# A chain of ten layers on one core: bias rows copied 64 times instead of 128, one more piece of a down projection kept back, and weight remainders moved behind a norm's rows

## The reference, cut to what matters

```python
def mixer_layer(x, ...):                       # twice
    h = rmsnorm(x, g_norm); z = h @ w_in
    o_a = diff_attention(dq, dk, dv, lam, rel_bias[:, :8])     # score + bias[bucket(k - q)]
    o_b = dilated groups, each with its own 4 bias heads       # 12 more bias heads
    o_m = memory_attention(mq, *(rmsnorm(mem, g_mem) @ w_mem_kv))
    return x + merged(o_a, o_b, o_m) @ w_out
def second_block(x, c, ...):
    for i in range(4):                          # mixers: swa, gla, fox, swa
        sh1, sc1, g1, sh2, sc2, g2 = split(silu(c) @ ada_w[i] + ada_b[i])
        x = x + g1 * mixer(modulate(rmsnorm_2(x, gain), sh1, sc1))
        h = modulate(rmsnorm_2(x, gain), sh2, sc2)
        x = x + g2 * ((silu(h @ w_g) * (h @ w_u)) @ w_down)    # 2816 inner columns
    return rmsnorm_2(x, final_norm)
```

## Time and profile before

| | |
|---|---|
| median of 3 runs | 2226.8 us (2224.5 to 2227.19) |
| the profiled execution | 2226.34 us; its span 2224.5 us |
| PE busy | 2135.0 us (96%) |
| DVE, ACT, POOL busy | 70%, 48%, 8% |
| granted TensorE clock, mean | 0.992 of full |
| DMA | 475.61 MB, mean 214 GB/s |

### The profile page before, as it was taken

How to read it: one execution, slowest core, us unless ns; L and a number is a source line. 1 busy time by engine, 2 the same in 40 slices (tenths; PEclk the granted TensorE clock), 3 DMA queues, 4 the chain that set the end, 5 groups by cost and what they waited for, 6 DMA issues and landing times. The chain is left out here.

```text
span 2224.5 us, 34008 instructions
## 1 busy us (share of the span) xinstructions
PE 2135.0 (96%) x13635; PEld 1901.5 (85%) x13635; DVE 1566.2 (70%) x2153; ACT 1078.5 (48%) x2082; POOL 184.7 (8%) x204
## 2 busy tenths in 40 slices
PE   7899999999999999999999998999999999999997
PEld 6799888878988888777999787899798899788996
DVE  6477657776776677666899677899645895667444
ACT  5354546544445555455445543454555454464342
POOL 1000000201000011011001001001000001111000
PEclk9999999999999999999999999999999999999999
DMA  9987744566876455634899434799644797425651
GB/s 303 286 260 249 242 144 147 174 229 232 258 252 225 138 164 179 217 106 130 292 348 356 162 129 142 235 363 364 208 133 143 255 355 259 150 94 177 201 182 67
DMA packets 297171, 475.61 MB, mean 214 GB/s; under 512 B 20001, under 2 KB 151531, under 8 KB 297013
## 3 DMA queue, kind: packets, MB, share of 16 engines
q1 hardware_dynamic: 286708, 441.20, 58.8%
q0 software_dynamic: 10304, 32.23, 5.0%
HBM read 465.88 MB, written 7.47 MB: 213 GB/s over the span
## 5 line engine op out<-in xcount | busy, mean ns | idle before, releaser
L150 DVE TENSOR_TENSOR wlo<-raw,whi 128x1024 fp32r<-128x1024 f32 x640 | 771.3, 1232 | 217.5 <-ACT whi L144 215.5
L144 ACT ACTIVATE whi<-raw 128x1024 fp32r<-128x1024 f32 x640 | 649.1, 1056 | 198.6 <-DMA raw<-in_ffn_w_gu 64.9
L138 PE MATMUL G<-HTh,whi 128*128 128x256 f32 x2336 | 671.7, 288 | 11.2 <-ACT pool L144 7.0
L138 PE MATMUL G<-HTh,wlo 128*128 128x256 f32 x2336 | 661.9, 283 | 0.0
L138 PE MATMUL G<-HTl,whi 128*128 128x256 f32 x2336 | 661.8, 283 | 0.0
L138 PEld LDWEIGHTS G<-HTh,whi 128*128 128x128 f32 x2336 | 448.7, 192 | 20.0 <-issue 9.7
L138 PEld LDWEIGHTS G<-HTl,whi 128*128 128x128 f32 x2336 | 448.9, 192 | 2.1
L138 PEld LDWEIGHTS G<-HTh,wlo 128*128 128x128 f32 x2336 | 448.7, 192 | 0.0
L144 ACT ACTIVATE pool<-G 128x128 f32<-128x128 f32 (+2 forms) x400 | 165.3, 434 | 507.2 <-PE G L138 449.8
L138 PE MATMUL G<-whi,HTh 128*128 128x512 f32 (+1 forms) x784 | 314.2, 401 | 24.8 <-DVE wlo L150 14.0
L138 PE MATMUL G<-whi,HTl 128*128 128x512 f32 (+1 forms) x784 | 304.3, 388 | 5.1 <-DVE HTl L158 4.8
(11 more groups left out here) (193 smaller groups left out, 2233.7 us busy)
## 6 DMA issues: line engine op xcount, KB each, us to landing
raw<-in_ada_w SPq DMA_DIRECT2D x192, 512.0 KB, 6.2
raw<-in_ffn_w_gu SPq DMA_DIRECT2D x352, 256.0 KB, 5.1
raw<-in_w_in SPq DMA_DIRECT2D x128, 512.0 KB, 4.6
raw<-in_ffn_w_down SPq DMA_DIRECT2D x88, 512.0 KB, 6.8
raw<-in_w_in SPq DMA_DIRECT2D x160, 256.0 KB, 4.6
raw<-in_swa_w_in SPq DMA_DIRECT2D x24, 512.0 KB, 5.2
pool<-mod_rows POOLq DMA_DIRECT2D x24, 512.0 KB, 6.2
raw<-in_gla_w_in SPq DMA_DIRECT2D x24, 512.0 KB, 5.0
```

The lines of the kernel that those rows point to most:

```text
L138: return self.e.matmul(out, a, b, start=start, stop=stop, skip_group_check=True) if self.e else self
L144: return self.e.activation(out, a, func, bias=bias, scale=scale, accum_out=accum) if self.e else self
L150: return self.e.tensor_tensor(out, a, b, op) if self.e else self
```

## The change: what it does

Four edits. (1) The bias table is written 64 times, and each bias tile is read by two transfers of 64 rows. (2) In a feed-forward the second down piece of unit 8 is kept back as well: `down(8)` does one piece, and `part` does the other, and no part of t = 1 stands any longer between those of t = 0; 30 matmuls of t = 1 are left behind the last one of t = 0. The stream brings the four pieces in the order that this needs, and `turning` counts from unit 8, which moves some `ada_w` pieces forward. (3) In `normed`, `rest()` and `refill` stand behind the new rows. (4) `mod_rows` is put off when all four PSUM banks of its kind are held.

```diff
-        self.scratch = nc.dram_tensor("bias_scratch", (20, P, 512), F32, kind="Internal").ap()
+        self.scratch = nc.dram_tensor("bias_scratch", (20, 64, 512), F32, kind="Internal").ap()
...
-            for kc in range(2):
-                res.append(("w", ("dn", l, v), [("dn", 0, I["ffn_w_down_2"][l][v * 256 + kc * P:v * 256 + kc * P + P, :])]))
+            for w, kc in {8: [(8, 0)], 9: [(8, 1), (9, 0), (9, 1)]}.get(v, [(v, 0), (v, 1)]):
+                res.append(("w", ("dn", l, w), [("dn", 0, I["ffn_w_down_2"][l][w * 256 + kc * P:w * 256 + kc * P + P, :])]))
...
-    return (name in ("ya", "wo", "wo2") and last == 1 or name == "dn" and last > 8 or name == "gu" and last == 0
+    return (name in ("ya", "wo", "wo2") and last == 1 or name == "dn" and last > 7 or name == "gu" and last == 0
...
-            if kk == 4 and self.modq:
+            if kk == 4 and self.modq and not all(self.gheld):
...
             self.xtok[t] = N.nx[t] + N.sq[t]
-            q, have = self.mean(t, N)
-            self.rest()
-            self.refill(4 + t)
-            r, tr = self.rstd(q, have)
+            r, tr = self.rstd(*self.mean(t, N))
...
+            self.rest()
+            self.refill(4 + t)
             if t:
...
-        self.scr.append(self.load("POOL", f"scr{k}", self.M.scratch[:, 32 * k:32 * k + 32, :],
-                                  self.btb.a[0:20, :].unsqueeze(1).to_broadcast([20, 32, 512]), [self.tbt, self.step]))
+        self.scr.append(self.load("POOL", f"scr{k}", self.M.scratch[:, 16 * k:16 * k + 16, :],
+                                  self.btb.a[0:20, :].unsqueeze(1).to_broadcast([20, 16, 512]), [self.tbt, self.step]))
...
+            evs = [(f"bias{r}", (u.name, i, k)) for k in range(2)]
+            for k in range(2):
+                src = bass.AP(self.M.scratch.tensor, h * 64 * 512 + 127 - 64 * k, [[511, 64], [1, 384]])
+                self.h_bias(r, 64 * k, src, self.scr, self.bias_free[r], evs[k])
...
-            for kc in range(2):
+            for kc in range(1 if v == 8 else 2):
                 n, lo = self.take(("dn", l, v))
...
-                for kc in range(2):
+                for kc in range(v == 8, 2):
...
-        last = ([part(0, 9, (0, 1)), part(1, 9, (0,)), part(0, 10, (0,)), part(0, 10, (1,))], [part(1, 9, (1,))],
-                [part(1, 10, (0,)), part(1, 10, (1,), l < 3)])
+        last = ([part(0, 8, (0, 1)), part(0, 9, (0, 1)), part(0, 10, (0,)), part(0, 10, (1,))], [part(1, 8, (0, 1))],
+                [part(1, 9, (0, 1)), part(1, 10, (0,)), part(1, 10, (1,), l < 3)])
```

More of the change, by code:

```diff
@@ L1112, in get_bias @@
             r = self.bias_at.pop(0)
[L1113 to L1116, removed]
+            evs = [(f"bias{r}", (u.name, i, k)) for k in range(2)]
+            for k in range(2):
+                src = bass.AP(self.M.scratch.tensor, h * 64 * 512 + 127 - 64 * k, [[511, 64], [1, 384]])
+                self.h_bias(r, 64 * k, src, self.scr, self.bias_free[r], evs[k])
+            u["bias"].append((r, evs[1]))
     def biased(self, u):
@@ L3245, in h_gate, with h_bias @@
         e.tensor_tensor(m, m, gq, ALU.add).then_inc(*self.up(added))
-    def h_bias(self, r, src, scr, free, ev):
+    def h_bias(self, r, p, src, scr, free, ev):
         e = self.e
@@ L3250, in h_bias @@
             e.wait_ge(*self.at(t))
-        e.dma_start(self.M.bias_t[:, r, :], src).then_inc(*self.up(ev, 16))
+        e.dma_start(self.M.bias_t[p:p + 64, r, :], src).then_inc(*self.up(ev, 16))
     def h_rope(self, ps, t, dst, nh, tmp, cb, full, trp, free, read, done):
```

## The result

The changed kernel takes 2235.8 us (median of 4 runs, 2234.9 to 2237.6), the kernel before in the same rounds 2225.8 us (4 runs, 2224.5 to 2227.2). The ratio is 1.0038, with a 95% interval of 1.0025 to 1.0050: slower by 10.0 us. The forecast was 2228.4 us, a gain and a loss that cancel to +2.1 us. The time lies within its range (2215 to 2237), but on the side that had a chance of 0.27, and outside the range that the prediction gave for its likeliest case alone (2222 to 2234).

A forecast was written before the change was run, and what follows sets the result against it. TensorE is busy 96%, so only its waits and lower clock count. Terms -9.3 + 6.0 + 1.2 + 2.4 + 4.0 - 2.2 = +2.1 us on 2226.3 give 2228.4 us; 8-in-10 range 2215 to 2237.

The forecast's parts named there:

- likeliest case: The forecast itself: start gain and turn losses nearly cancel, 2228.4 us, own range 2222 to 2234; chance 0.38.
- The start: Weight waits at 77.36 and 85.71 us and the slow stretch vanish with half the bias writes: -9.3 us net.
- The wait at 61.61: At the start, TensorE's 0.90 us wait for late VectorE stays and grows by about 0.7 us.
- The start wins nothing: Rival at the start: DMA engines stay full as weights take the free time; 2237.7 us, chance 0.12.
- half of the start: Rival at the start: only 6 to 7 us of the saving reaches the late pieces; 2231.4 us, chance 0.12.
- The remainder behind the rows: Turns into a feed-forward: TensorE's awaited remainder starts 2.3 us later, 0.8 comes back; +1.5 each, +6.0 over four.
- no slow clock: Rival in turns out of a feed-forward: waits of 4.4 us pass at full clock; 2222.7 us, chance 0.18.
- The kept piece: Three turns out of a feed-forward: 2.25 us wait goes, 4.4 us comes at head's third piece; +2.4, clock +4.0.
- The turns are free: Rival: postponed remainders aren't what TensorE meets last, so turns lose nothing; 2209 us, or 2214.8 breaking even; chance 0.20.
- The end: Final norm: t = 0's chain starts 2.7 us earlier relative to TensorE's end, less 0.4 for the late remainder; -2.2 us.
- I take nothing: Doubled bias reads on GpSimd stand in gaps between roots and cost nothing; bounds 0 to +2 us.

The follow-up runs named there:

- The experiment on the two halves: Changed kernel, but remainders behind the norm's rows only for the first 128 tokens, ahead of the root for the second 128: 2218.8 us, ratio 0.9964.
- the one with 58: Kernel with copies at steps 8, 18, 24, 30 and last-layer kept piece, its 40 bias reads moved from GpSimd to SyncE: 2227.2 us, ratio 0.9994.
- the changed kernel without part three: Changed kernel with `normed` as before, remainders ahead of the rows again: 2219.0 us, ratio 0.9948; run again 2217.4 us, ratio 0.9957.

## Why the prediction was right, and where it wasn't

**The start** was right: both waits and the slow stretch are gone, 10.0 us against 9.3. GpSimd's queue gave back 52.7 - 29.7 = 23.0% of 55 us of the engines, 12.7 us; half of the bias was put at 13. The wait at 61.61 grew by 0.77 us (0.7 was said), and it grows by edit three alone: the bias by itself won 11.4 us. *The start wins nothing* and *half of the start* are out. So the upper end of the range, 2237, came from a rival that failed (the start without gain), and that 2235.8 lies under it is luck.

**The remainder behind the rows** was right in mechanism and in its wait. Said: rows 0.88 us after the mean, the wait 3.2 us, 0.8 us back at HTl. Measured: 0.88, 3.02, and 0.87 us back. The experiment on the two halves shows that the step behind the second half's rows is the cause. Its term was too small for the clock: the sentence "for the turns into a feed-forward, where the wait grows to about 3.2 us, I take nothing, bounded by 1.7 us each above". In feed-forward 0's turn the offset grows by 2.1 us over the wait and by 1.5 us over the six matmuls and the transposes behind it, at half clock. Four turns cost 9.8 us, not 6.0, with the clock of 2034 to 2038 at 0.57 in the last of them. This is the term that missed by most, and *no slow clock* is out with it.

**The kept piece** was right as far as it goes: the wait ahead of the transposes is gone, 4.18 us stand at the head's third piece (said 4.4), with half clock behind them, and the three turns cost 8.0 us against 6.4 with their clock. The slow stretch behind the last of them runs on over 1932 to 1939. What the prediction didn't separate is whose loss that is. It worked out the kept piece in the presence of the moved remainders; without these the same edit costs 0.9 to 2.7 us over its three turns and wins 2.0 us net at the end, nothing in all (1.0000). *The turns are free* is false of the change and nearly true of this edit by itself.

**The end** won 2.0 us in the changed kernel, against 2.2: 2.6 from the last matmul on, less 0.6 ahead of it, where the late remainder stands (0.4 was said).

**The step that failed** is "I take nothing" for the doubled reads. Their cost was looked for on GpSimd's row in front of the roots, where there is none, and bounded at 0 to +2. It stands behind the last instruction, in the DRAIN whose row was in the trace of before (8.12 us, at 98 transfers): +3.0 us, above the bound. Each of six kernels with 138 transfers has 11.14 us, the one with 58 has 5.42.

**By chance or not foreseen**: 1.6 us at half clock in fox's attention, behind a wait of 0.78 us that the kernel before has as well, at full clock there. It came in the changed kernel, in the one with 64 copies and a kept piece in the last layer, in the one with doubled reads alone and in the one with copies at steps 8, 18, 24 and 30, and in none of the other nine profiles. So no edit goes with it, and what decides it is open.

The four differences, +3.0 for the DRAIN, +3.8 for the turns in, +1.6 for those out and +1.6 in the attention, less 0.7 at the start and 0.1 for the rest, make the 9.2 us between +2.1 and +11.3. The forecast was 7.4 us under the median. The lowest median here is that of a version without the edit that loses: 64 copies and the piece kept back in the last layer, 2216.6 us. The other three with 64 copies and the second half's remainders ahead of the rows lie within 2.4 us of it.

## What to carry to other kernels

Work moved behind a chain is late by the whole chain: before a producer's step is put off, look whether the consumer already waits for it in the trace. If it does, the price is the chain's length, and, where the wait grows to 3 or 4 us, the time at half clock behind it as well. An edit that adds small transfers on GpSimd's queue is paid at the end of the program too, here 0.075 us for each, so look at the last DRAIN. And transfers that crowd out weights are cheaper to shrink than to reschedule: moved later, they kept a buffer that the next result needed, or met each other.

## What the runs showed of the hardware

- GpSimd's last DRAIN grows with the number of transfers that GpSimd issued in the whole program, most of them landed long before: 5.42 us at 58, 8.12 at 98, 11.14 at 138. Their size doesn't matter: 138 with 128 copies and 138 with 64 give the same 11137 ns. The point at 58 lies 0.3 us above the line through the other two.
- A root of 128 values on GpSimd takes 0.56 us with VectorE idle and 1.47 us while VectorE subtracts a remainder beside it. The second root of the turn into swa's layer, before and then with the remainders moved away (GpSimd in order of time):

```profile
952.20 1.46 POOL L150 TENSOR_TENSOR sm<-sm,mhalf 128x1 f32<-128x1 f32 x1 [2.86 <-DVE sm L155]
```

```profile
942.58 0.55 POOL L150 TENSOR_TENSOR sm<-sm,mhalf 128x1 f32<-128x1 f32 x1 [2.86 <-DVE sm L155]
```

  The Trainium skill, in "SBUF — State Buffer", section "SBUF: two separate sides", has VectorE and GpSimd share one pair of ports. By it, a VectorE instruction with two inputs in SBUF and a GpSimd instruction that reads SBUF can't use the pair at once: the one that starts first holds it for its whole instruction, and the other is blocked. The rows agree: the subtraction reads `raw` and `whi`, it starts 0.17 us ahead of the root of 952.20 and ends at 953.25, and the root ends 0.41 us behind it, at 953.66.
- With copies of 1.31 MB under way, a megabyte through GpSimd's queue took the DMA engines twice the time of one through SyncE's beside it (54.6% for 5.37 MB, 35.3% for 6.88 MB), with copies of 0.66 MB and other transfers about the same (29.7% for 4.85 MB, 58.3% for 10.30 MB). The cause is open.
- The clock behind a wait isn't given by the wait's length alone: in the turn out of feed-forward 0 a wait of 2.10 us for the third piece had matmuls at half clock behind it in the kernel with the first half's remainders moved (from 1238.24 us), and none in the changed kernel without part three (from 1238.00 us).
- The kernels with 64 copies spread over 1.0 to 3.2 us from run to run (4 to 6 runs each), those with 128 and nine runs or more over 4.9 to 12.1 us. The number of runs differs too, so part of this can be the larger number. The start with large copies varies: three profiles with the same copies at the same steps stand at 0, 1.9 and 1.9 us at 130 us, and four with 64 copies, whose setup waits as before, from -11.2 to -11.7. So the start isn't shown to be the whole of the spread.
